# The opening of a transformer kernel: two weight sums in four blocks of feature chunks, with the first four panels' products between them

## The reference

```
shift, scale, gate = split(silu(c) @ w_ada[l] + b_ada[l], 3)          # latent row
shift_c, scale_c, gate_c = split(silu(c_ctx) @ w_ada[l] + b_ada[l], 3)  # context row
h_lat = rms_norm(x, g) * (1 + scale) + shift
h_ctx = rms_norm(ctx, g) * (1 + scale_c) + shift_c
p = h @ w_in                       # q, k, v, gates, low-rank parts: 37 panels of 128 columns
...                                # two attentions, then
x = x + gate * (y @ w_out)         # out-projection: 16 panels
```

## Time and profile before

| | |
|---|---|
| median of 3 runs | 3294.24 us (lowest 3286.79) |
| profiled execution: time / span | 3290.46 us / 3288.7 us |
| busy: PE, PEld, DVE, ACT, POOL | 90%, 70%, 76%, 36%, 21% of the span |
| transfers | 932.7 MB, 284 GB/s over the span |
| chain that ended last | PE 68%, DVE 10%, DMA 8%, POOL 6% |

### The profile page before, as it was taken

One profiled execution on the slowest core, in us unless ns is written; L12 is line 12 of the kernel. 1 busy time (PEld: TensorE's weight loads), 2 busy tenths in 40 slices (PEclk: granted clock), 3 DMA queues, 4 the chain that ended last, 5 costly groups with the idle time before them and its releaser, 6 DMA issues.

```text
span 3288.7 us, 38665 instructions
## 1 busy us (share of the span) xinstructions
PE 2973.2 (90%) x14668; PEld 2294.1 (70%) x14668; DVE 2492.4 (76%) x3464; ACT 1174.4 (36%) x1804; POOL 700.0 (21%) x748
## 2 busy tenths in 40 slices
PE   5899999999999999998999999999999996766666
PEld 1478887557778998588999899788888884222223
DVE  7888996655877886577654564898989996988886
ACT  1332323324234444145545554344444442111111
POOL 1000000000320000023000000222222214777772
PEclk9999999999999999999999999999999998978888
DMA  9555675252876785647443443999999999999996
GB/s 407 218 192 192 230 274 212 90 230 99 325 268 250 287 333 192 243 171 293 177 154 142 168 164 144 368 405 417 400 418 408 414 400 367 388 409 410 409 409 267
DMA packets 160232, 932.70 MB, mean 284 GB/s; under 512 B 21552, under 2 KB 42288, under 8 KB 53168
## 3 DMA queue, kind: packets, MB, share of 16 engines
q0 software_dynamic: 77568, 520.24, 40.1%
q1 hardware_dynamic: 68368, 384.82, 30.0%
q10 hardware_dynamic: 14112, 25.17, 2.0%
HBM read 900.80 MB, written 29.36 MB: 283 GB/s over the span
## 4 chain that ended last, share of the span: by engine, by line
PE 68%; DVE 10%; DMA 8%; POOL 6%; issue 5%; ACT 2%; DVEq 0%; SPq 0%; POOLq 0%; ACTq 0%
PE psum L1154 33%; PE psum L1099 17%; PE psum L1163 6%; DMA memh<-dots,memr 4%; PE psum L1305 3%; POOL memh L958 3%; DVE w_lo L1443 2%; POOL memr L970 2%; PE psum L1324 2%; PE psum L1123 2%; DMA memr<-in_panels_dram 2%; DMA memh<-in_panels_dram 1%; DVE psum L2405 1%; PE psum L1315 1%; ACT w_hi L1436 1%
## 5 line engine op out<-in xcount | busy, mean ns | idle before, releaser
L1443 DVE TENSOR_TENSOR w_lo<-memr,w_hi 128x1024 fp32r<-128x1024 f32 x614 | 743.7, 1233 | 325.5 <-ACT w_hi L1436 325.0
L1436 ACT ACTIVATE w_hi<-memr 128x1024 fp32r<-128x1024 f32 x614 | 642.9, 1057 | 866.9 <-PE psum L1154 366.4
L1154 PE MATMUL psum<-h_hi,w_hi 128*128 128x512 f32 (+1 forms) x1632 | 575.5, 353 | 5.2 <-DVE w_lo L1443 4.6
L1933 DVE CUSTOM_DVE_ANT_0 junk<-memr 128x2048 bf16<-128x2048 f32 x224 | 520.1, 2322 | 74.4 <-DMA memr<-in_ada_dram 54.0
L1154 PE MATMUL psum<-h_hi,w_lo 128*128 128x512 f32 (+1 forms) x1632 | 561.8, 344 | 0.0
L1154 PE MATMUL psum<-h_lo,w_hi 128*128 128x512 f32 (+1 forms) x1632 | 561.7, 344 | 0.0
L1099 PE MATMUL psum<-w_hi,l_hi 128*128 128x512 f32 x1024 | 400.2, 391 | 7.9 <-DVE w_lo L1443 7.0
L1099 PE MATMUL psum<-w_hi,l_lo 128*128 128x512 f32 x1024 | 399.4, 390 | 0.0
L1099 PE MATMUL psum<-w_lo,l_hi 128*128 128x512 f32 x1024 | 399.3, 390 | 0.0
L1346 PE MATMUL psum<-memr,memh 128*128 128x512 f32 x456 | 248.4, 702 | 166.0 <-ACT memh L1869 148.5
L1154 PEld LDWEIGHTS psum<-h_hi,w_hi 128*128 128x128 f32 x1632 | 310.4, 190 | 49.2 <-DVE w_lo L1443 6.4
(11 more groups left out here) (283 smaller groups left out, 4518.3 us busy)
## 6 DMA issues: line engine op xcount, KB each, us to landing
memr<-in_panels_dram SPq DMA_DIRECT2D x323, 1024.0 KB, 7.5
memr<-in_ada_dram POOLq DMA_DIRECT2D x168, 1024.0 KB, 5.3
memh<-in_panels_dram SPq DMA_DIRECT2D x16, 1024.0 KB, 23.4
dots<-sq ACTq DMA_DIRECT2D x64, 256.0 KB, 9.8
memh<-in_ada_dram POOLq DMA_DIRECT2D x8, 1024.0 KB, 15.8
memr<-in_xin_dram SPq DMA_DIRECT2D x1, 4096.0 KB, 40.7
gstore<-sq ACTq DMA_DIRECT2D x16, 256.0 KB, 4.7
memh<-gstore SPq DMA_DIRECT2D x2, 2048.0 KB, 7.3
```

Source lines behind the costliest of these rows:

```text
L1154: ins = pe.matmul(bank(o["bank"])[:, 0:o["w"]], w_[:, c, :], x_[:, kc, :], start=kc == 0 and j == 0, stop=kc == DC - 1 and j == 2)
L1436: act.activation(hi, a, ACT.Copy).then_inc(hi_ready, 1)
L1443: dve.tensor_tensor(lo_, a, hi.bitcast(F32), ALU.subtract).then_inc(lo_ready, 1)
L1933: chain(dve.tensor_tensor_reduce(junk[:, :], w, cact[:, v_, :], 1.0, 0.0, ALU.mult, ALU.add, mod[:, a, m:m + 1]))
```

## The change

The opening becomes one stage ("opening"). Both thirds, scale and shift, are now multiplied on PE, in four blocks of four feature chunks. A panel of `w_ada` now holds 512 rows x 512 columns of the matrix: block b needs four panels for its scale and four for its shift, 32 panels in all. Each panel is four matmuls whose stationary operand is 32 columns wide (two vectors, the rest zero) and whose outputs go to four different quarters of the 128 partitions of one bank; a matmul with a picking matrix adds the quarters and turns the row into columns. As soon as block b's columns are there, its four chunks are modulated, rounded and split. The first four panels of the in-projection (`quad`) are accumulated in four banks at once: between two panels of the next block PE runs one panel's products with the four chunks of this block. The last block's products follow the loop.

x comes first, in four transfers; all transfers of the opening are on SP's queue; the broadcast vectors come after the last `w_ada` panel, and their SiLU stands behind the fifth panel. The 16 shift chunks leave DVE. The other 160 chunks are spread anew: 42 in the in-projection (none behind the first five panels), 14 in the up-projection, 40 in the out-projection of layer 0. The head norms of the first panels come three panels later. The second block's vector is loaded and passed through SiLU one attention later.

The core of the diff:

```
-        spread(DC, 48, [1.0] * 17 + [1.4] * 18 + [0] * 2)
-        spread(DC + 37, 16, [1] * 6 + [0])
-        spread(DC + 44, 32, [1] * 14 + [0] * 2)
+        spread(COND, 42, [0] * 5 + [1.0] * 12 + [1.4] * 18 + [0] * 2)
+        spread(COND + 37, 14, [1] * 6 + [0])
+        spread(COND + 44, 40, [1] * 14 + [0] * 2)
...
+                elif st["kind"] == "opening":
+                    for b in range(BLOCKS):
+                        sp.dma_start(X0[:, 4 * b:4 * b + 4, :], x_all[:, 4 * b:4 * b + 4, :]).then_inc(x0_in[b], 16)
+                    for n in range(COND):
+                        if n == 4:
+                            sp.dma_start(consts[:, :], consts_d).then_inc(const_in, 16)
...
+                        if n == 8:
+                            for i in range(QUAD):
+                                load_panel(COND + i)
+                        if n >= COND_SLOTS:
+                            sp.wait_ge(cond_used, n - COND_SLOTS + 1)
+                        sp.dma_start(region(cond_at[n % COND_SLOTS], PANEL), panels[n]).then_inc(cond_in[n % COND_SLOTS], 16)
...
+            def rows(n):
+                b, kind, q = n // 8, n // 4 % 2, n % 4
+                pe.wait_ge(cond_in[n % COND_SLOTS], 16 * (n // COND_SLOTS + 1))
...
+                for g in range(4):
+                    ins = pe.matmul(bank(5 + kind)[32 * g:32 * g + 32, :], sc[:, 4 * q + g, :], w[:, g, :],
+                                    start=q == 0, stop=q == 3)
+                ins.then_inc(cond_used, 1)
...
+            def columns(b, kind):
+                pe.wait_ge(cond_row, 2 * b + kind + 1)
...
+                for j in range(4):
+                    ins = pe.matmul(bank(COND_BANKS[kind])[:, 2 * j:2 * j + 2], cond_rows[kind][:, P * j:P * j + P], con("pick", 2),
+                                    start=True, stop=True)
...
+            for b in range(BLOCKS - 1):
+                for j in range(4):
+                    rows(8 * (b + 1) + 2 * j)
+                    rows(8 * (b + 1) + 2 * j + 1)
+                    if j == 2:
+                        columns(b + 1, 0)
+                    products(quad[j], range(4 * b, 4 * b + 4))
+                    if j == 3:
+                        columns(b + 1, 1)
+            for o in quad:
+                products(o, range(12, 16))
...
+            for b in range(BLOCKS):
+                columns(b, 0)
+                if b == 2:
+                    dve_half(dve, quad[3], 1)
+                columns(b, 1)
+                modulate(4 * b)
+                modulate(4 * b + 2)
+                for c in range(4 * b, 4 * b + 4):
+                    remainder(c)
...
```

More of the change, by code:

```diff
@@ L99, in make_plan @@
 def make_plan():
-    panels = [(0, "ada", i) for i in range(DC)]
+    panels = [(0, "ada", i) for i in range(COND)]
     for layer in range(DEPTH):
@@ L221, in build @@
         const_in = sem("const_in")
+        cols_in = sem("cols_in")
+        x0_in = [sem(f"x0_in{i}") for i in range(BLOCKS)]
         cvec_in = sem("cvec_in")
@@ L360, in norm, with opening @@
             return st
+        def opening(gr):
+            gr.update(sq0=totals["sq"], ms=totals["ms"])
+            totals["sq"] += DC
+            totals["ms"] += 1
+            totals["xh"] += DC
+            totals["xl"] += DC
+            totals["xn"] += DC // 2
+            totals["md"] += DC // 2
+            return stage("opening", group=gr, engines=("pe", "act", "dve"))
         def inside(st, groups, panels_of):
@@ L370, in inside @@
                 gr.update(sq0=totals["sq"], ms=totals["ms"], sw=totals["swap"], made=[by_step[i] for i in made])
+                made = [i + gr.get("later", 0) for i in made]
                 ready_at = made[-1]
@@ L437, in build @@
             if layer == 0:
[L438 to L445, removed]
+                begun = opening(dict(x=[X[:, c, :] for c in range(DC)], w=D, hi=[h_hi[:, c, :] for c in range(DC)],
+                                     lo=[h_lo[:, c, :] for c in range(DC)], streams=both, rt=sq[:, 2, :]))
+            else:
+                stage("scale", g="norm_g", gi=DC, a=ADA0[1], streams=(CTX, LAT), engines=("dve",), seam=True)
+                norm([dict(x=[X[:, c, :] for c in range(DC)], w=D, y=[H[:, c, :] for c in range(DC)],
+                           hi=[h_hi[:, c, :] for c in range(DC)], lo=[h_lo[:, c, :] for c in range(DC)],
+                           streams=both, a=ADA0[1], summed=summed)])
             def in_proj(p, at, q=q, k=k, vT=vT, v=v, kr=kr, cq=cq, ckv=ckv, lo=lo):
@@ L461, in build @@
             st = gemm(g, 37, in_proj)
+            if layer == 0:
+                begun["next"], st["quad"], st["ahead"] = st, QUAD, 2 * QUAD
             g += 37
@@ L470, in build @@
             groups, made = of_q + of_k + of_kr, q_made + k_made + [range(kr0, kr0 + 1)]
+            if layer == 0:
+                for gr in of_q + of_k:
+                    gr["later"] = QUAD - 1
             if layer:
@@ L515, in build @@
             stage("load_g", x=G2, chunks=(8, 16), engines=("sp",))
+            if layer == 0:
+                stage("load_c2", engines=("sp",))
             def mla_kq(h, q=q, kn=kn, qr=qr, kr=kr):
@@ L930, in _ @@
             added = 0
-            for n in range(DC, N_ADA - DC):
+            for n in range(N_ADA - 2 * DC):
                 o = first_chunk.get(n - 2)
@@ L1277, in stats @@
             def stats(gr):
[L1278 removed]
+                if not gr.get("summed"):
                     pe_stats(pe, gr)
```

368 lines of the change are left out of this document (213 added, 155 removed).

## The result

The changed kernel takes 3300.47 us (median of 6 runs, 3297.31 to 3303.79) against 3292.8 of the kernel before on the same chip: ratio 1.0029, interval [1.0017, 1.0041]. That is no change by the 2% mark, but a loss that the interval tells from zero, where 3291 was forecast. One of the six executions of the kernel before took 7747.60 us; it is left out of the ratio, and the other five have a median of 3291.35. The profiled execution took 3299.47 us (span 3297.7), 9.0 more in span than before.

The account below looks back on a forecast made before the run. PE was taken to bound the projections, only just, with DVE's three-chunk panels longer. Opening -33.4, moved sums +1.7, up-projection +1 and out-projection +31 gave +0.3 on the profiled 3290.46: 3291 us, range 3264 to 3316.

Parts of the forecast that it names:

- The out-projection: Layer 0's out-projection: twelve three-chunk panels at 14.04 us on DVE are no longer covered by PE; +31 us.
- PE waits about 3 us a panel: Layer 0's out-projection: PE waits about 3 us a panel and can lose nothing more by it.
- the slack of 4: End of layer 0's out-projection: before, PE needed the second-to-last half's w_lo some 4 us after it was made.
- The opening: Opening: PE, not transfers, sets the quad's end at 134.3; panel five starts at 137.0 instead of 170.41, -33.4 us.
- First block: starts at 48: Opening's first block: starts at 48, paced by eight panels (20 us) and the last pair's products, ends 70.5.
- Narrow price: Opening: four narrow matmuls of one weight panel cost 0.64 us, with ends 0.43 (all at once) and 1.72 (one after another).
- switches: Opening: each switch between narrow and wide loads costs about 0.5 us, eight per block, 4.0 us.
- The rival of queueing products: Opening: narrow products queue at 1.72 us a panel, panel five starts at 157.6; +21, 3311 us; chance 0.17.
- The begin wait: Before panel five: its first half is split with PE idle after the quad, 2.7 us.
- the moved sums: After panel five's start: two sums of squares of 0.86, formerly before it, now come later; +1.7 us.
- the up-projection: Up-projection: three double-chunk panels behind its second panel take 15 us of DVE; +1 us (0 to +5).
- the rivals: Queue 3311 (0.17), no interleaving 3311 (0.05), free out-projection 3260 (0.14), overlap without drain 3281 (0.12).

Follow-up runs that it names:

- the three kernels that leave the opening alone: Changed kernel with 32 out-projection chunks, with POOL's reload before the square sum, or with half-chunk loads there: 3268.34, 3305.24 and 3284.89 us.
- the kernel on one quarter: Changed kernel with all four narrow matmuls of a w_ada panel accumulated on the same 32 partitions: 3357.39 us, ratio 1.0196 to the kernel before.
- With 32 chunks: Changed kernel with 32 instead of 40 w_ada chunks in layer 0's out-projection, eight moved to layer 1: 3268.34 us, ratio 0.9935 to the kernel before.

## Why the prediction was wrong

**The out-projection: right.** Forecast +31. PE's end of the stage moved by 7.2 + 24.9 = +32.1. The pair of `w_lo` that I placed 35.4 later came 35.7 later (971.71 - 633.33 against 960.95 - 658.26), and the slack of 4 was 3.6. DVE's twelve long panels set the stage's length, as forecast. PE's loss came otherwise than in "PE waits about 3 us a panel": the twelve waits range from 0.2 to 3.4 and sum to 24.3, and the rest is longer products. Behind the wait of 3.2 that ends at 864.05 the mean granted clock was 0.79 until 877.93 (1.00 is the higher of its two levels, 2.4 GHz, and 0.50 the lower); that panel took 13.9 for 11.0, and the next wait was 0.2. PE had that time, so the forecast's length holds. My reading of the earlier trace rows was half right only: the reload stands behind the square sum, but that costs some 0.5 us of 14; the wait behind it comes from two slots and 5.5 us from issue to landing.

**The opening: the step "First block: starts at 48" failed.** Its products start late. The ninth panel's narrow products start at 51.30 instead of 48, and the block ends at 75.7, not 70.5. The next two blocks win back 1.8 of these 5.2 (they end at 98.5 for 93.8 and 122.8 for 119.4), the last one loses 0.8 again (the quad at 138.5 for 134.3). So the miss of 4.2 comes in with the first block:

```profile
51.30 1.93 PE L1310 MATMUL psum<-memh,junk 128*32 128x512 f32 x8 [7.90 <-DMA memh<-in_panels_dram]
53.79 1.93 PE L1310 MATMUL psum<-memh,junk 128*32 128x512 f32 x8 [0.56 <-DMA memh<-in_panels_dram]
55.65 0.80 PE L1334 MATMUL psum<-h_hi,w_hi 128*128 128x512 f32 x1
```

I let the ninth panel land when 18.9 MB were moved, at 428 GB/s. By 51.30 the queue had moved 24 x 379 + 21 x 401 + 6.3 x 422 = 20.2 MB (422 is the rate from 45 to 70): 1.3 MB of it belonged to transfers in flight beside that panel, and 24 to 45 ran at 401. The first is worked out from rows, not tried; moving the issue earlier showed no clear gain. In the three kernels that leave the opening alone the same products start at 50.30, 49.75 and 51.40, so 1.8 to 3.4 us of lateness come back each time.

The sum also had no term for the clock. PE did nothing from 45.00 to 51.30; the granted clock was 0.50 in that time and up to 55.60, the lower of its two levels, and the first twelve products took 3.79 for the 2.96 of the next twelve (from start to end 3.9 here, 4.9 to 5.0 in those three kernels). The last block starts behind a wait of 2.85: the clock was 0.57 from 125.50 to 129.50, and the 48 products took 12.9 (125.64 to 138.55) for 10.9. That is some 2.8 us, which cheaper switches and shorter waits partly paid.

**Narrow price and switches: two errors that cancelled.** I read x8 in the earlier trace rows as eight matmuls; they are two records each of four. So 3.59 is the price of one panel one after another, as the kernel on one quarter showed (3.5), and the bounds were 0.9 and 3.6, not 0.43 and 1.72. The price was 0.93 for 0.64. A switch was 0.1 for 0.5. A pair with its products came to 4.81 for 5.0, so the blocks' lengths nearly held. The Trainium skill's rule that a change of tiling mode drains the engine ("TensorEngine Tiling (Array Packing)", Key Properties) is not refuted, but the trace does not agree with my price for it: what the 0.86 and 0.76 of the earlier trace rows were stays open. The rival of queueing products, priced at 3311, would have been 3357.

**The begin wait, the moved sums, the up-projection: right in size.** 2.65 for 2.7; two sums of 0.86 now behind panel five (2.0 for 1.7); +2.3 for +1, inside 0 to +5.

**What no step had: +4.7 behind the out-projection.** From PE's end to the next stage's long run pass 41.74 for 37.06. First before, then after, the end of the stage on PE and DVE:

```profile
971.44 1.02 PE L1056 MATMUL psum<-sq,ones 128*128 128x512 f32 x2
973.23 1.13 PE L1059 MATMUL psum<-sq,ones 128*128 128x512 f32 x2 [0.77 <-ACT sq L1490]
```

```profile
978.60 1.02 PE L1096 MATMUL psum<-sq,ones 128*128 128x512 f32 x2
983.47 2.07 PE L1099 MATMUL psum<-sq,ones 128*128 128x512 f32 x2 [3.85 <-ACT sq L1573]
```

```profile
979.65 1.06 ACT L1515 ACTIVATE w_hi<-memr 128x1024 fp32r<-128x1024 f32 x1 [3.19 <-DMA memr<-in_panels_dram]
```

```profile
980.74 1.23 DVE L1522 TENSOR_TENSOR w_lo<-memr,w_hi 128x1024 fp32r<-128x1024 f32 x1 [2.77 <-ACT w_hi L1515]
981.88 0.87 DVE L2131 SCALAR_TENSOR_TENSOR memr<-psum,mod,memr 128x256 f32<-128x256 f32 x2
```

PE ends at 978.60, but the gated add of its last output (L2131) stands on DVE behind the look-ahead split of a later panel, and that split waits for a load. The load's buffer came free with the delayed pair at 971.71. So the last square, the mean and the norm start 3.1 us later than before. Before, PE ended the stage 10.5 us after that pair (960.95), long enough for the load to land; now it ends 6.9 us after it. With 32 chunks the wait is back to 0.77. I followed the late `w_lo` to PE and stopped there; what else the same pair releases was late next. The other 1.6 go with PE's clock: the mean's two records stand behind a wait of 3.85 for 0.77, in a stretch with a granted clock of 0.50 (983.47 to 985.60) where it was 1.00 before the change, and last 2.07 for 1.13; the interleaved products of the next two panels (84 in the chain) take 21.07 for 20.42.

**The sum.** 4.2 from the opening, 1.6 from sums and up-projection, 1.1 from the out-projection and 4.7 behind it, less 2.8 that later stages gave back: 8.8 above the forecast's +0.3, against +9.0 measured. The sign was lost in the first block and behind the out-projection, where the prediction had no term; none of the rivals came true. That 3291 lay below the median of before was no step's doing: +0.3 was added to a profiled execution that stood 3.8 under that median.

## What to carry to other kernels

A stage that PE only just bounds has no room for work moved into it: eight more chunks cost 32 to 36 us in a place where 32 of them had been nearly free, and the same chunks in later projections cost almost nothing. With two slots, a third use per period waits out what the second use leaves of a load's time from issue to landing (here 3.06 of 5.52); look at that time before the order of the queue that issues it. Price the first products behind a wait at the clock that was granted there. And where a stage ends late, follow every instruction that queues behind the late one on each engine, beyond the engine that was being watched.

## What the runs showed of the hardware

Four float32 matmuls with 32 stationary columns each, on four quarters of the output partitions, took 0.93 us together and 3.5 us on one quarter.

A chunk's reduction that starts while POOL adds squares lasts 3.12 us (853.87, the add ends at 854.84); one that starts before the add lasts 2.28 (854.07, the add begins at 854.99). The 0.84 is nearly the rest of the add. The add shows the same from its side: it lasts 2.59 when it starts inside a reduction (852.25, the reduction ends at 853.69), and 1.29 while DVE is idle, as in the kernel before:

```profile
964.83 1.29 POOL L923 TENSOR_TENSOR sq<-sq 128x512 f32<-128x512 f32 x1 [2.55 <-ACT sq L1490]
```

The Trainium skill ("SBUF — State Buffer", SBUF: two separate sides) says that DVE with two inputs from SBUF and POOL lock each other out for a whole instruction; by that rule, the trace agrees.

A load of half the bytes landed 1.65 us sooner, of 5.52; by these two some 5.52 - 2 x 1.65 = 2.2 us of a load beside the kernel's other transfers do not go with its bytes (an estimate from the two kernels).
